# Feed-forward entry: the first two weight blocks interleaved by rows of tiles, squares summed in pairs before the matrix engine

## The chip, the cores and the metric

The kernel runs on one core of a Trainium2 chip, as one launch. The metric is the device time of that launch in microseconds. All times here are of this kernel on this kind of chip.

## The reference, cut to what matters

The program is a two-layer trunk with three sub-layers per layer: a feed-forward (F1), a token mixer, and a second feed-forward (F2). All three start with a norm of the residual stream and end with another. The change touches only how a feed-forward starts.

```
def rmsnorm(x, g):
    y = xf * lax.rsqrt(jnp.mean(xf * xf, axis=-1, keepdims=True) + RMS_EPS)
    return (y * g.astype(jnp.float32)).astype(x.dtype)
def swiglu(x, wg, wu, wd):
    return (jax.nn.silu(x @ wg) * (x @ wu)) @ wd
for l in range(DEPTH):                      # DEPTH = 2
    h = swiglu(rmsnorm(x, ffn1_pre_g[l]), ffn1_wg[l], ffn1_wu[l], ffn1_wd[l])
    x = x + 0.5 * rmsnorm(h, ffn1_post_g[l])
    m, new = token_mix(rmsnorm(x, mix_pre_g[l]), l, ...)
    x = x + rmsnorm(m, mix_post_g[l])
    h = swiglu(rmsnorm(x, ffn2_pre_g[l]), ffn2_wg[l], ffn2_wu[l], ffn2_wd[l])
    x = x + 0.5 * rmsnorm(h, ffn2_post_g[l])
```

The model width is 1024, the feed-forward width 2816, and there are T = 320 tokens (256 of a prompt, 64 of samples). Everything is float32.

## The kernel before, in words

**Layout.** The residual `x` lies in on-chip memory transposed: 8 tiles of 128 rows (channels) by 320 columns (tokens). A weight block is 128 x 2048 numbers, which is 8 tiles along the input channels (k = 0 to 7) times 256 output channels (two halves, c = 0 and 1). Blocks are streamed through two buffers `raw[0]` and `raw[1]` by the SP queue, each load waiting until the block before in the same buffer was used up (`lo_ready`).

**Split numbers.** A product of two float32 numbers is made of three products of a reduced format: high weights by high input, high weights by low input, low weights by high input. ScalarE (ACT) rounds a block to its high part `whi[s]` (`split_hi`, counted by `hi_ready`), VectorE (DVE) subtracts to get the low part `wlo[s]` (`split_lo`, counted by `lo_ready`). Likewise ACT writes `uh` (x times gain, rounded; `high_input`) and DVE writes `ul` (the rest; `low_input`). A feed-forward block is thus 16 tiles (c, k) by 3 = 48 matmuls of TensorE (PE) into the two PSUM banks `dps[:, 2s]` and `dps[:, 2s + 1]`.

**The norm is applied late.** The inputs `uh`, `ul` are not yet divided by the root of the mean square. ACT also writes the squares of x into `u` (`square`, two tiles at a time, counted by `sq_ready`). PE multiplies them by a matrix of ones into `mx[:, 3]` (`pre_sum`, line 659: two matmuls of ordinary float32 after each group of tiles, eight in all). The last one signals `sum_done`; ACT takes the root (`root`), DVE takes the reciprocal (`scale`, line 1480) and only then scales what came out of the first block (`times_scale`, line 1422).

**The entry of a feed-forward.** The inputs come in four groups j = 0 to 3 of two tiles, because DVE and ACT are still making them (`border` and `enter`: DVE scales and adds the sub-layer before to x, ACT rounds, DVE subtracts). PE works on block 0 in the order of the groups: for each j, wait for `u_ready`, 12 matmuls, then `pre_sum`. After all of block 0 it takes block 1, 48 matmuls, then a loop over the other upper blocks (2 to 21), then 12 lower ones. While PE is in block 1, the following chain runs for block 2, in this order on DVE: `scale`, `times_scale` of block 0's result, `split_lo` of block 2. PE may start block 2 when that last one is done. Four entries occur in the program: F1 and F2 of both layers. Between the last matmul of the sub-layer before and an entry, `keep_busy` issues 11 matmuls whose result is not used.

**Engines wait by semaphores alone**; every engine's order is the order of the code. POOL's queue waits for the `sum_done` of F1 to start loading small weights and the first halves of blocks for the mixer.

Of the kernel before, what the change touches and what calls it, by code (L numbers as in the profile page):

```python
# [27 lines left out]
ALU = mybir.AluOpType  # L28
# [3 lines left out]
P = 128  # L32
D = 1024
KD = D // P
# [4 lines left out]
T = TP + NB * TS  # L39
# [13 lines left out]
NFF = 2 * (B_A - B_F1)  # L53
# [93 lines left out]
def trunk(nc, xT, wstream, smallw, params, logits, consts, st_shift, st_rwkv, st_lru, st_conv, st_hgrn,  # L147
          yT, o_shift, o_rwkv, o_lru, o_conv, o_hgrn):
    ctx = ExitStack()
    with ctx:  # L150
# [212 lines left out]
        def wait_turn(eng, l, g):  # L363

            eng.wait_ge(S["turn_done"], l * NTURN + (g + 1))

        def landed(l, pair):

            return (l * NLOAD + pair - ((B_G0 - B_B) // 2 if 2 * pair >= B_G0 else 0)) * 16 + 16
# [170 lines left out]
        def _(pe):  # L540
# [7 lines left out]
            def pair_wait(l, qhalf, s):  # L548

                pe.wait_ge(pair_free[s], l * (NPAIR // 2) + qhalf + 1)  # L550
# [99 lines left out]
            def keep_busy(n):  # L650

                for _ in range(n):
                    pe.matmul(mx[:, 2, 0:2 * P], ident, cst[:, 0:2 * P], start=True, stop=True)

            def pre_sum(l, idx, j):

                pe.wait_ge(S["sq_ready"], l * 24 + (4 * idx + j + 1))
                for k in (2 * j, 2 * j + 1):
                    m = pe.matmul(mx[:, 3, 0:T], ones, u[:, k, :], start=k == 0, stop=k == KD - 1,  # L659
                                  skip_group_check=True)  # L660
                if j == 3:
                    m.then_inc(S["sum_done"], 1)

            def added_sum(l, idx):

                pe.wait_ge(S["sq_added"], l * 3 + (idx // 2 + 1))
                pe.matmul(mx[:, 3, 0:T], ones, sq[:, 0, :], start=True, stop=False, skip_group_check=True)

            def next_sum(l, idx):
# [18 lines left out]
            def split_tiles(s, kt, hi, lo_, half, first=True, last=True, k0=0, norm=None, ends=None):  # L688
# [6 lines left out]
                for c, k, j in order:  # L695
# [14 lines left out]
                    if norm and c == 1 and k == 2 * j + 1:  # L710
                        pre_sum(norm[0], 2 * norm[1], j)

            def ffn(l, b, q, f):
                def split_in(i, j):

                    pe.wait_ge(S["lo_ready"], l * NFF + i * 2 + (B_A * f + j + 3))

                for s in range(2):
                    split_in(0, s)
                    pair_wait(l, q // 2, s)  # L720
                    split_tiles(s, KD, uh[:, :, :], ul[:, :, :], s, norm=None if s else (l, 2 * f))
                with pe.Fori(1, KF // 2) as i:
                    for s in range(2):
                        split_in(i, s)
                        pair_wait(l, i + q // 2, s)
                        split_tiles(s, KD, uh[:, :, :], ul[:, :, :], s)
                for j in range(12):
                    half, part = j // 3, j % 3
                    pe.wait_ge(S["lo_ready"], l * NFF + (B_A * f + KF + j + 3))
                    if part == 0:  # L730
                        pair_wait(l, (q + KF + half) // 2, half % 2)

                    pe.wait_ge(S["h_ready"], l * 22 + (11 * f + 1 + (4, 8, 11)[part]))
                    split_tiles(j % 2, 8 if part < 2 else 6, hfh, hfl, half % 2, first=part == 0, last=part == 2,
                                k0=8 * part, ends=(l, 4 * f + 1) if j == 11 else None)
                post_sum(l, 4 * f + 1)
# [680 lines left out]
        def _(dve):  # L1417
            def tt(out, a, b, op):
                return nc.vector.tensor_tensor(out, a, b, op)  # L1419
# [84 lines left out]
            def add_squares(l, idx, j):  # L1504
# [6 lines left out]
                if j == 2:  # L1511
                    m.then_inc(S["sq_added"], 1)

            def border(l, idx, step, following):

                def scaled(j):

                    k = slice(2 * j, 2 * j + 2)
                    times_scale(ho[:, k, :], ho[:, k, :])
                    fence()  # L1520

                def renew(k):

                    return stt(x[:, k, :], ho[:, k, :], step, x[:, k, :], ALU.mult, ALU.add)

                scale(l, idx)
                for k in range(2):
                    mul(ho[:, k, :], ho[:, k, :], rs[:, :])
                    fence()
                    renew(k).then_inc(S["x_new" if k else "x_first"], 1)  # L1530
                for j in range(4):
                    if j == 0 and following:
                        low_input(*following, j, lambda: scaled(1))
                    else:
                        if j < 3:
                            scaled(j + 1)
                        if following:
                            low_input(*following, j)
                    if j < 3:
                        renew(slice(2 * j + 2, 2 * j + 4)).then_inc(S["x_new"], 1)  # L1540

            def split_lo(l, f, i, j, s):

                dve.wait_ge(S["hi_ready"], l * NFF + i * 2 + (B_A * f + j + 1))
                tt(wlo[s][:, :], raw[s][:, :], whi[s][:, :].bitcast(F32), ALU.subtract).then_inc(S["lo_ready"], 1)
# [426 lines left out]
            for l in range(L):  # L1972
                nc.vector.tensor_copy(prm[:, :], tile_at(prm_all, l)).then_inc(S["prm_ready"], 1)
                if l == 0:
                    for j in range(4):
                        low_input(0, 0, "ffn1_pre_g", j)
                    split_lo(0, 0, 0, 0, 0)
                ffn(l, B_F1, 0)
                if l == 0:
                    dve.wait_ge(S["const_loaded"], 16)  # L1980
# [215 lines left out]
```

## Time and profile before

| what | us |
|---|---|
| median of 3 runs | 2083.63 |
| lowest and highest of them | 2079.86, 2084.89 |
| the profiled execution, its time | 2080.08 |
| the profiled execution, its span | 2078.3 |
| TensorE busy in it | 2037.3 (98%) |
| VectorE busy in it | 1379.3 (66%) |
| ScalarE busy in it | 797.3 (38%) |

The span is from the first to the last instruction of the profiled execution; 1.8 us of its time lie around it. In rows of the profile a matmul is shown with its full duration, but the next one starts before it ends; the useful number is the distance from start to start.

### The profile page before, as it was taken

To read this page: it belongs to the slowest core of one execution; us is meant where nothing else is said; L and a number is where in the kernel's file an instruction comes from. 1 tells how busy PE (TensorE), PEld (TensorE's weight loads), DVE (VectorE), ACT (ScalarE), POOL (GpSimd) and SP (SyncE) were. 2 spreads that over 40 slices of the span, in tenths; PEclk is the share of its full clock that TensorE was granted. 3 is DMA by queue.
4 is the path that set the end of the run, shared out by engine and by line. 5 is a ranking of instruction groups with operands and counts; after the bars stand their busy time and mean duration, and the time that the engine had idled before them with its cause. 6 is when DMAs were issued, how large, how long until landed. Compare 5 with 4: busy or idle time off the path is not lost.

```text
span 2078.3 us, 31983 instructions
## 1 busy us (share of the span) xinstructions
PE 2037.3 (98%) x12928; PEld 1868.1 (90%) x12928; DVE 1379.3 (66%) x2053; ACT 797.3 (38%) x940; POOL 86.1 (4%) x164
## 2 busy tenths in 40 slices
PE   7999999999999999999999999999999999999998
PEld 6999989888877798999999998989887778989998
DVE  5776487877667676555377755877874676766544
ACT  4444463333243244233354444623323323443332
POOL 1111000000000000000011100000000000000000
PEclk9999999999999999999999999999999999999999
DMA  6887423333332342444458864323333333434442
GB/s 239 304 308 266 172 107 108 113 113 112 125 122 104 123 174 102 143 160 151 167 193 309 297 241 160 129 88 113 113 113 132 107 122 143 142 115 148 161 146 102
DMA packets 60826, 326.66 MB, mean 157 GB/s; under 512 B 7249, under 2 KB 7441, under 8 KB 34481
## 3 DMA queue, kind: packets, MB, share of 16 engines
q1 hardware_dynamic: 43200, 262.92, 35.9%
q0 software_dynamic: 17520, 62.27, 8.2%
q8 instruction: 75, 1.23, 0.2%
q14 instruction: 31, 0.25, 0.0%
HBM read 290.81 MB, written 34.36 MB: 156 GB/s over the span
## 4 chain that ended last, share of the span: by engine, by line
PE 92%; DVE 4%; DVEq 1%; ACT 1%; DMA 1%; issue 1%; SPq 0%
PE dps L703 44%; PE dps L607 11%; PE dps L557 10%; PE dps L642 6%; PE mx L803 2%; PE mx L817 2%; PE mx L813 2%; PE mx L917 2%; PE mx L659 1%; PE dps L630 1%; DMA raw<-in_wstream 1%; DVE ho L1422 1%; PE mx L933 1%; PE mx L760 1%; PE mx L970 1%; PE mx L947 1%
## 5 line engine op out<-in xcount | busy, mean ns | idle before, releaser
L1047 ACT ACTIVATE whi<-raw 128x2048 fp32r<-128x2048 f32 (+1 forms) x144 | 269.1, 1869 | 486.2 <-PE dps L703 465.0
L1419 DVE TENSOR_TENSOR wlo<-raw,whi 128x2048 fp32r<-128x2048 f32 x136 | 311.7, 2292 | 210.2 <-ACT whi L1047 205.2
L703 PE MATMUL dps<-uh,whi 128*128 128x320 f32 x1408 | 430.3, 306 | 19.6 <-DVE wlo L1419 15.0
L703 PE MATMUL dps<-uh,wlo 128*128 128x320 f32 x1408 | 434.3, 308 | 0.0
L703 PE MATMUL dps<-ul,whi 128*128 128x320 f32 x1408 | 432.9, 307 | 0.0
L703 PEld LDWEIGHTS dps<-uh,whi 128*128 128x128 f32 x1408 | 264.8, 188 | 25.1 <-issue 18.4
L703 PEld LDWEIGHTS dps<-uh,wlo 128*128 128x128 f32 x1408 | 264.8, 188 | 0.0
L703 PEld LDWEIGHTS dps<-ul,whi 128*128 128x128 f32 x1408 | 264.0, 187 | 0.6
L607 PE MATMUL dps<-u,raw 128*128 128x320 f32 x768 | 234.5, 442 | 0.0
L703 PE MATMUL dps<-hfh,whi 128*128 128x320 f32 x704 | 220.4, 313 | 0.0
L703 PE MATMUL dps<-hfh,wlo 128*128 128x320 f32 x704 | 217.6, 309 | 0.0
L703 PE MATMUL dps<-hfl,whi 128*128 128x320 f32 x704 | 216.7, 308 | 0.0
L642 PE MATMUL dps<-nh,parts 128*128 128x320 f32 x704 | 211.0, 342 | 0.0
L607 PEld LDWEIGHTS dps<-u,raw 128*128 128x128 f32 x768 | 137.9, 191 | 50.6 <-issue 5.3
L703 PEld LDWEIGHTS dps<-hfl,whi 128*128 128x128 f32 x704 | 133.2, 189 | 0.6
L703 PEld LDWEIGHTS dps<-hfh,whi 128*128 128x128 f32 x704 | 132.3, 188 | 0.6
L703 PEld LDWEIGHTS dps<-hfh,wlo 128*128 128x128 f32 x704 | 132.0, 187 | 0.0
L642 PEld LDWEIGHTS dps<-nh,parts 128*128 128x128 f32 x704 | 126.8, 189 | 4.1 <-issue 2.9
L1047 ACT ACTIVATE tmp<-mx 128x640 f32<-128x640 f32 (+2 forms) x80 | 47.4, 592 | 194.8 <-PE mx L803 127.7
L1422 DVE TENSOR_TENSOR ov<-dps,ov 128x640 f32<-128x640 f32 x52 | 42.8, 823 | 71.9 <-PE dps L703 65.9
L1047 ACT ACT_TABLE_LOAD x64 | 82.1, 1283 | 2.1 <-PEq L2177 0.7
L1422 DVE TENSOR_TENSOR ov<-dps,rs 128x640 f32<-128x640 f32 x56 | 46.2, 824 | 54.3 <-PE dps L703 45.3
(321 smaller groups left out, 3493.3 us busy)
## 6 DMA issues: line engine op xcount, KB each, us to landing
raw<-in_wstream SPq DMA_DIRECT2D x198, 1024.0 KB, 4.8
u<-in_wstream POOLq DMA_DIRECT2D x44, 512.0 KB, 7.1
split_store<-wha POOLq DMA_DIRECT2D x44, 512.0 KB, 7.6
raw<-in_wstream SPq DMA_DIRECT2D x44, 512.0 KB, 4.1
parts<-split_store SPq DMA_DIRECT2D x44, 512.0 KB, 5.0
hs<-in_st_hgrn POOLq DMA_DIRECT2D x8, 512.0 KB, 5.6
out_o_hgrn<-hs POOLq DMA_DIRECT2D x8, 512.0 KB, 2.9
out_yT<-x SPq DMA_DIRECT2D x2, 1280.0 KB, 4.5
```

The costliest lines, as they stand in the source:

```text
L557: m = pe.matmul(out, w[:, k, n0:n0 + P], v[:, k, :], start=first and i == 0, stop=last and i == 2, skip_group_check=True)
L607: m = pe.matmul(dps[:, 2 * s + c, 0:T], w[:, k, c * P:(c + 1) * P], u[:, k, :], start=k == 0, stop=k == KD - 1, skip_group_check=True)
L630: m = pe.matmul(dps[:, 2 * (b % 2) + c, 0:T], w[:, k, c * P:(c + 1) * P], u[:, k, :], start=k == 0, stop=k == KD - 1, skip_group_check=True)
L642: m = pe.matmul(dps[:, 2 * (b % 2) + c, 0:T], w[:, k % 4, c * P:(c + 1) * P], v, start=k == 0 and t == 0, stop=k == KD - 1 and t == 2, ski ...
L703: m = pe.matmul(dps[:, 2 * half + c, 0:T], w[:, k, c * P:(c + 1) * P], v[:, k0 + k, :], start=first and k == 0 and i == 0, stop=last and k ...
L803: m = pe.matmul(mx01[:, c * P:(c + 1) * P], ao[li % 2][:, c, :], tinv[:, c, :], start=True, stop=True)
L813: m = pe.matmul(mx23[:, c * P:(c + 1) * P], tinvt[:, c, :], zs[:, c, :], start=True, stop=True)
L817: m = pe.matmul(product_at(li, c), zs[:, c, :], tinvt[:, c, :], start=True, stop=True)
L917: m = pe.matmul(mx[0:b - a, (li + 1) % 2, a:b], kss[li % 2][:, a:b], qps[li % 2][:, a:b], start=True, stop=True)
L1047: return nc.scalar.activation(out, in_, f, **kw)
L1419: return nc.vector.tensor_tensor(out, a, b, op)
L1422: return nc.vector.tensor_tensor(out, a, b, ALU.mult)
```

## The change

Block 0 and block 1 are worked on together at the entry of every feed-forward, by the new function `entry`. After group j of block 0 (12 matmuls), PE does the same group of block 1 with the high weights only (8 matmuls: 4 tiles by `uh` and `ul`). The low weights of block 1 (16 matmuls) come after all of that. The sums of squares are no longer made from eight tiles: DVE first adds two tiles of `u` to one (`add_pair`, signalled by `sq_added`), and PE multiplies only the four results by ones (`pair_sum`), one after group 1 of block 0, one after group 2, two after group 3. Numbers counted by `sq_added` elsewhere are shifted to fit.

```
--- before.py
+++ after.py
@@ -363,6 +363,14 @@
         def wait_turn(eng, l, g):
 
             eng.wait_ge(S["turn_done"], l * NTURN + (g + 1))
+
+        def pair_added(l, idx, j):
+
+            return l * 11 + ((0, 6)[idx // 4] + j + 1)
+
+        def post_added(l, idx):
+
+            return l * 11 + {1: 5, 3: 6, 5: 11}[idx]
 
         def landed(l, pair):
 
@@ -652,6 +660,13 @@
                 for _ in range(n):
                     pe.matmul(mx[:, 2, 0:2 * P], ident, cst[:, 0:2 * P], start=True, stop=True)
 
+            def pair_sum(l, idx, j):
+
+                pe.wait_ge(S["sq_added"], pair_added(l, idx, j))
+                m = pe.matmul(mx[:, 3, 0:T], ones, u[:, 2 * j, :], start=j == 0, stop=j == 3, skip_group_check=True)
+                if j == 3:
+                    m.then_inc(S["sum_done"], 1)
+
             def pre_sum(l, idx, j):
 
                 pe.wait_ge(S["sq_ready"], l * 24 + (4 * idx + j + 1))
@@ -663,7 +678,7 @@
 
             def added_sum(l, idx):
 
-                pe.wait_ge(S["sq_added"], l * 3 + (idx // 2 + 1))
+                pe.wait_ge(S["sq_added"], post_added(l, idx))
                 pe.matmul(mx[:, 3, 0:T], ones, sq[:, 0, :], start=True, stop=False, skip_group_check=True)
 
             def next_sum(l, idx):
@@ -710,15 +725,48 @@
                     if norm and c == 1 and k == 2 * j + 1:
                         pre_sum(norm[0], 2 * norm[1], j)
 
+            def entry(l, q, f):
+
+                tiles = [[v[s][:, :].rearrange("p (k n) -> p k n", k=KD) for v in (whi, wlo)] for s in range(2)]
+
+                def part(s, c, k, w, v, first, last):
+
+                    return pe.matmul(dps[:, 2 * s + c, 0:T], tiles[s][w][:, k, c * P:(c + 1) * P], v[:, k, :],
+                                     start=first, stop=last, skip_group_check=True)
+
+                pe.wait_ge(S["lo_ready"], l * NFF + (B_A * f + 3))
+                pair_wait(l, q // 2, 0)
+                for j in range(4):
+                    ks = (2 * j, 2 * j + 1)
+                    for c, k in [(c, k) for k in ks for c in range(2)] if j == 0 else [(c, k) for c in range(2) for k in ks]:
+                        if c == 0 and (k == 2 * j or k == 1):
+                            u_wait(l, 2 * f, k)
+                        part(0, c, k, 0, uh, k == 0, False)
+                        part(0, c, k, 0, ul, False, False)
+                        m = part(0, c, k, 1, uh, False, k == KD - 1)
+                    if j == 3:
+                        m.then_inc(S["block_done"], 1)
+                    if j == 0:
+                        pe.wait_ge(S["hi_ready"], l * NFF + (B_A * f + 2))
+                        pair_wait(l, q // 2, 1)
+                    for i in (() if j == 0 else (j - 1,) if j < 3 else (2, 3)):
+                        pair_sum(l, 4 * f, i)
+                    for c in range(2):
+                        for k in ks:
+                            part(1, c, k, 0, uh, k == 0, False)
+                            part(1, c, k, 0, ul, False, False)
+                pe.wait_ge(S["lo_ready"], l * NFF + (B_A * f + 4))
+                for c in range(2):
+                    for k in range(KD):
+                        m = part(1, c, k, 1, uh, False, k == KD - 1)
+                m.then_inc(S["block_done"], 1)
+
             def ffn(l, b, q, f):
                 def split_in(i, j):
 
                     pe.wait_ge(S["lo_ready"], l * NFF + i * 2 + (B_A * f + j + 3))
 
-                for s in range(2):
-                    split_in(0, s)
-                    pair_wait(l, q // 2, s)
-                    split_tiles(s, KD, uh[:, :, :], ul[:, :, :], s, norm=None if s else (l, 2 * f))
+                entry(l, q, f)
                 with pe.Fori(1, KF // 2) as i:
                     for s in range(2):
                         split_in(i, s)
@@ -1511,6 +1559,11 @@
                 if j == 2:
                     m.then_inc(S["sq_added"], 1)
 
+            def add_pair(l, n, j):
+
+                dve.wait_ge(S["sq_ready"], l * 24 + (8 * n + j + 1))
+                tt(u[:, 2 * j, :], u[:, 2 * j, :], u[:, 2 * j + 1, :], ALU.add).then_inc(S["sq_added"], 1)
+
             def border(l, idx, step, following):
 
                 def scaled(j):
@@ -1538,6 +1591,10 @@
                             low_input(*following, j)
                     if j < 3:
                         renew(slice(2 * j + 2, 2 * j + 4)).then_inc(S["x_new"], 1)
+                    if following and following[1] != 1 and j:
+                        add_pair(*following[:2], j - 1)
+                if following and following[1] != 1:
+                    add_pair(*following[:2], 3)
 
             def split_lo(l, f, i, j, s):
 
@@ -1975,6 +2032,8 @@
                     for j in range(4):
                         low_input(0, 0, "ffn1_pre_g", j)
                     split_lo(0, 0, 0, 0, 0)
+                    for j in range(4):
+                        add_pair(0, 0, j)
                 ffn(l, B_F1, 0)
                 if l == 0:
                     dve.wait_ge(S["const_loaded"], 16)
```

The rows below are the program's instruction order on one engine. A name as `dps<-uh,whi` is the tile written and the tiles read, `mx<-u,cst` is a sum of squares by ones. First PE, at the end of block 0 of a feed-forward's entry before the change:

```order
L703 MATMUL dps<-uh,wlo 128x320
L659 MATMUL mx<-u,cst 128x320 [waits sq_ready]
L659 MATMUL mx<-u,cst 128x320
L703 MATMUL dps<-uh,whi 128x320 [waits pair_free1,lo_ready]
L703 MATMUL dps<-ul,whi 128x320
```

The last two rows begin block 1, whose 48 matmuls all stand behind the last sum. PE at the same place in the change, from the end of group 3 of block 0 to the start of block 2:

```order
L734 MATMUL dps<-uh,wlo 128x320
L666 MATMUL mx<-u,cst 128x320 [waits sq_added] x2
L734 MATMUL dps<-uh,whi 128x320
L734 MATMUL dps<-ul,whi 128x320
L734 MATMUL dps<-uh,whi 128x320
L734 MATMUL dps<-ul,whi 128x320
L734 MATMUL dps<-uh,whi 128x320
L734 MATMUL dps<-ul,whi 128x320
L734 MATMUL dps<-uh,whi 128x320
L734 MATMUL dps<-ul,whi 128x320
L734 MATMUL dps<-uh,wlo 128x320 [waits lo_ready]
L734 MATMUL dps<-uh,wlo 128x320 x15
```

Behind the last sum there now stand 8 matmuls with high weights and 16 with low ones, and then block 2; the other 24 of block 1 have moved ahead of it. The new wait in the entry is at the first group of block 1, which needs its high weights. PE in the change, from the end of group 0 of block 0:

```order
L734 MATMUL dps<-uh,wlo 128x320
L734 MATMUL dps<-uh,whi 128x320 [waits pair_free1,hi_ready]
L734 MATMUL dps<-ul,whi 128x320
L734 MATMUL dps<-uh,whi 128x320
L734 MATMUL dps<-ul,whi 128x320
L734 MATMUL dps<-uh,whi 128x320
L734 MATMUL dps<-ul,whi 128x320
L734 MATMUL dps<-uh,whi 128x320
L734 MATMUL dps<-ul,whi 128x320
L734 MATMUL dps<-uh,whi 128x320 [waits u_ready]
```

Where two sums stood between the groups, eight matmuls of block 1 stand now. On DVE at the program's start, the rows before the change:

```order
L1419 TENSOR_TENSOR wlo<-raw,whi 128x2048 [waits hi_ready] x2
L1480 RECIPROCAL rs<-rt 128x320 [waits rt_ready]
L1422 TENSOR_TENSOR ov<-dps,rs 128x640 [waits block_done]
L1419 TENSOR_TENSOR wlo<-raw,whi 128x2048 [waits hi_ready]
L1422 TENSOR_TENSOR ov<-dps,ov 128x640 [waits block_done,silu_ready]
```

and in the change:

```order
L1467 TENSOR_TENSOR wlo<-raw,whi 128x2048 [waits hi_ready]
L1467 TENSOR_TENSOR u<-u 128x320 [waits sq_ready] x4
L1467 TENSOR_TENSOR wlo<-raw,whi 128x2048 [waits hi_ready]
L1528 RECIPROCAL rs<-rt 128x320 [waits rt_ready]
L1470 TENSOR_TENSOR ov<-dps,rs 128x640 [waits block_done]
L1467 TENSOR_TENSOR wlo<-raw,whi 128x2048 [waits hi_ready]
```

The four additions stand between the low weights of block 0 and those of block 1; the reciprocal, the scaling and the low weights of block 2 keep their order. At the other three entries two of the four additions stand between the steps that make the inputs, and two right ahead of the low weights of block 1.

## Rows read from the trace of the kernel before

**Rows 1.** The page: busy time by engine, and the chain that ended last.

```profile
PE 2037.3 (98%) x12928; PEld 1868.1 (90%) x12928; DVE 1379.3 (66%) x2053; ACT 797.3 (38%) x940; POOL 86.1 (4%) x164
...
PE 92%; DVE 4%; DVEq 1%; ACT 1%; DMA 1%; issue 1%; SPq 0%
```

**Rows 2.** Waits of PE: in total us, times, longest.

```profile
PE dps L703 <- DVE wlo L1419: 15.0, 1, 15.0
PE dps L703 <- DVE ul L1425: 4.6, 9, 0.8
```

**Rows 3.** Timeline of PE, third entry (F1, layer 2): start, us, instruction.

```profile
1046.82 1.24 PE L659 MATMUL mx<-u,cst 128*128 128x320 f32 x4
1048.67 0.41 PE L703 MATMUL dps<-uh,whi 128*128 128x320 f32 x1 [0.61 <-DVE ul L1425]
1048.92 0.31 PE L703 MATMUL dps<-ul,whi 128*128 128x320 f32 x1
...
1056.19 1.24 PE L659 MATMUL mx<-u,cst 128*128 128x320 f32 x4
1057.41 0.31 PE L703 MATMUL dps<-ul,whi 128*128 128x320 f32 x1
...
1064.21 0.30 PE L703 MATMUL dps<-uh,whi 128*128 128x320 f32 x1
```

**Rows 4.** Timelines of ACT and DVE around the same entry.

```profile
1053.13 0.72 ACT L1047 ACTIVATE u<-x 128x640 f32<-128x640 f32 x1
1057.47 0.53 ACT L1047 ACTIVATE rt<-mx,epst 128x320 f32<-128x320 f32 x1 [3.61 <-PE mx L659]
...
1041.90 0.49 DVE L1422 TENSOR_TENSOR ho<-ho,rs 128x320 f32<-128x320 f32 x1
...
1047.60 1.01 DVE L1425 SCALAR_TENSOR_TENSOR ul<-x,prm_all,uh 128x320 fp32r<-128x320 f32 x2 [0.34 <-ACT uh L1047]
...
1050.43 1.01 DVE L1425 SCALAR_TENSOR_TENSOR ul<-x,prm_all,uh 128x320 fp32r<-128x320 f32 x2 [0.35 <-ACT uh L1047]
...
1054.33 2.28 DVE L1419 TENSOR_TENSOR wlo<-raw,whi 128x2048 fp32r<-128x2048 f32 x1
1058.03 2.15 DVE L1480 RECIPROCAL rs<-rt 128x320 f32<-128x320 f32 x1 [1.42 <-ACT rt L1047]
1060.25 0.82 DVE L1422 TENSOR_TENSOR ov<-dps,rs 128x640 f32<-128x640 f32 x1
1060.99 2.28 DVE L1419 TENSOR_TENSOR wlo<-raw,whi 128x2048 fp32r<-128x2048 f32 x1
```

**Rows 5.** Timelines of PE, ACT and DVE at the first entry (program start).

```profile
27.97 0.55 PE L703 MATMUL dps<-uh,whi 128*128 128x320 f32 x1
28.36 0.31 PE L703 MATMUL dps<-ul,whi 128*128 128x320 f32 x1
...
30.37 1.90 ACT L1047 ACTIVATE whi<-raw 128x2048 fp32r<-128x2048 f32 x1
...
32.30 2.29 DVE L1419 TENSOR_TENSOR wlo<-raw,whi 128x2048 fp32r<-128x2048 f32 x1 [0.27 <-ACT whi L1047]
```

**Rows 6.** Third entry, later: ACT and DVE for blocks 4 and 5.

```profile
1072.61 1.92 ACT L1047 ACTIVATE whi<-raw 128x2048 fp32r<-128x2048 f32 x1 [6.23 <-DMA raw<-in_wstream]
...
1074.56 2.29 DVE L1419 TENSOR_TENSOR wlo<-raw,whi 128x2048 fp32r<-128x2048 f32 x1 [2.40 <-ACT whi L1047]
...
1082.53 2.29 DVE L1419 TENSOR_TENSOR wlo<-raw,whi 128x2048 fp32r<-128x2048 f32 x1
```

**Rows 7.** Windows in the mixer: PE, PEld, DVE, ACT, POOL, granted clock, DMA, GB/s.

```profile
708.50:711.90 3.40, 3.40 (x23) 2.46 (x21) 1.22 (x1) 0.00 (x0) 1.03 (x2) 1.00 0.46 193
711.95:715.36 3.41, 3.41 (x10) 2.48 (x10) 0.00 (x0) 2.05 (x3) 0.00 (x0) 0.50 0.44 173
```

**Rows 8.** Timeline of PE from 711.6 us on.

```profile
711.62 1.14 PE L947 MATMUL mx<-tmp,hs 128*128 128x8 f32 x6
712.60 3.22 PE L607 MATMUL dps<-u,raw 128*128 128x320 f32 x6
```

## The prediction

> **What bounds the kernel now.** I read the page first: TensorE is busy 98% of the span and is 92% of the chain that ended last [rows 1]. Then the waits of PE: apart from 15.0 us before its first matmul, the largest group is 4.6 us in nine waits for `ul`, the low inputs that VectorE makes at the entries [rows 2]; no wait for low weights occurs behind the first one. So PE bounds nearly everything, and an edit is worth what it takes from PE's own stream or from a wait there, unless it makes a new wait. Then I read the timeline of PE at the third entry, which the second and fourth repeat to 0.1 us with other offsets. The reader is to see in it three things. The four passes of a pair of sums take the place from 1056.19 to 1057.41 - 0.145 = 1057.27, so 1.08 us, or 0.54 us for one sum [rows 3]. Matmuls of split numbers follow each other in (1064.21 - 1057.41) / 47 = 0.145 us [rows 3], so a block of 48 is 6.95 us. And after group 0 PE stands until 1048.67, because the low inputs of group 1 come then; the stream goes on as if it had begun at 1048.92 - 0.145 = 1048.78 [rows 3]: a restart costs 0.17 us from what released it, low inputs that end at 1047.60 + 1.01 = 1048.61 [rows 4].
>
> The last view is the chain that runs beside block 1. The last sum ends at 1057.27; root at 1057.47, reciprocal at 1058.03, scaling at 1060.25, low weights of block 2 from 1060.99 to 1063.27 [rows 4]. That is 6.01 us from sum to weights. PE has 6.95 us of block 1 to do meanwhile and begins block 2 at 1064.21, so this chain has a slack of only 0.9 us. At the first entry it is longer: the last sum ends at 28.36 - 0.145 = 28.21, ACT loads a table first and has the high weights of block 2 at 32.27, the low ones end at 34.59 [rows 5], which is 6.38 us; the slack is 0.6.
>
> **The change part by part.** *The sums.* Four of eight go: 4 x 0.54 = 2.15 us less of PE per entry, 8.6 us for four.
>
> *Filling the wait after group 0.* Two sums (1.08 us) are replaced by 8 matmuls (1.16), so PE comes free at 1047.98 and still waits to 1048.78. That hides 0.1 us of the stall and no more, since the waited-for tiles do not come earlier.
>
> *The additions on VectorE.* No row shows this very operation. The nearest is a product of 128x320 at 0.49 us [rows 4]. Below, nothing, where VectorE waits anyway; above, four times 0.49 = 2.0 us per entry if all lay on the path. I take 0.1 us of effect on the inputs: the first addition stands between the renewal of x and the next scaling, and pushes the inputs of group 2, ready at 1051.4 now [rows 4], to 1051.6. PE comes to group 2 at 1052.2 in the new order (below), so this is covered by 0.6 us. The other three move the low weights of block 1 from 1054.33 to about 1055.3, done at 1057.6 [rows 4]; PE wants them only at 1059.6. The last squares are there at 1053.85 [rows 4], so the last addition is done by 1055.3 and its sum, at 1057.4, does not wait either. Without these covers an addition would cost its 0.49. The new wait for high weights of block 1 costs nothing: in ACT's code order they stand ahead of the inputs (`split_hi` before `enter`).
>
> *PE in the new order, third entry.* From 1048.78: group 1 of block 0 (12 x 0.145 = 1.74) to 1050.52, a sum to 1051.06, 8 of block 1 (1.16) to 1052.22; group 2 to 1053.96, sum to 1054.50, 8 to 1055.66; group 3 to 1057.40, two sums to 1058.48. Here is the step on which all rests: the last sum now ends 1.2 us later than before (1057.27), since 24 matmuls (3.48 us) of block 1 have moved ahead of it and only 2.15 us of sums and 0.1 of stall went. Behind it stand 8 + 16 = 24 matmuls, to 1061.96. That would be the gain, 2.25 us.
>
> *The chain.* It still needs 6.01 us from the last sum, now with 3.48 us of PE's work beside it and not 6.95. The low weights of block 2 are ready at 1058.48 + 6.01 = 1064.49, and with the restart of 0.17 block 2 begins at 1064.66, where it began at 1064.21. So PE stalls 2.7 us, the 2.25 are all given back, and 0.45 us more. At the first entry the last sum moves by 3.48 - 2.15 = 1.33 to 29.55, weights at 35.93, block 2 at 36.10 where it was 28.21 + 6.95 = 35.17: 0.93 us more, with a stall of 3.1. Sum over four entries: 0.93 + 3 x 0.45 = 2.3 us slower.
>
> *What is late next.* At the third entry the load of block 4 is issued behind the low weights of block 2, and ACT waits for it until 1072.61; from there VectorE has no slack, so that the low weights of block 5 end at 1084.82 [rows 6], 0.24 before PE's block 5 (1064.21 + 3 x 6.95 = 1085.06). If the load moves with its issue by 1.2 us, block 5 starts at 1086.02 + 0.17 and not at 1085.06 + 0.45: 0.7 us more. Bounds are nothing (if the load's lateness belongs to this execution) and 0.7; I take 0.7. Behind that VectorE follows PE. The queue of POOL, which waits for the same sum in F1, starts 1.2 to 1.3 us later; what it loads is for the mixer, and the waits of PE name none of it. Sum: 3.0 us.
>
> *The clock.* The trace before has no stall of PE as long as 2.7 us once it runs, so what one does to the granted clock is not seen. It has one fall: in 711.95 to 715.36 the granted clock is 0.50, which is 1.2 GHz and not 2.4, and in the stretch ahead, at 1.00, PE ended with a series of matmuls of 8 columns [rows 7, 8]. In the low stretch six float32 matmuls take 3.22 us [rows 8], some 0.53 each, where they take 0.27 at full clock [rows 3]: PE does half of its work, and 3.41 us at half cost 1.7. PE was never idle there, it only had little to stream; a stall of 2.7 us has nothing to stream. Bounds per stall: nothing, and 1.7 us; for four stalls nothing to 6.8. Since a mere thinning of the stream was enough once, I take it that the clock falls after about two of the four stalls, one of them partly under the stall itself: 2.5 us.
>
> The Trainium skill speaks to this (TensorE: Matmul & The Clock Gate, "HAM oscillation — how this bites in real kernels"): it names a length of idle gap below which the clock is not expected to fall, and the stalls worked out here are shorter. By that rule the sum would be 3.0 us; by the row of the fall it is 5.5. No row here shows a gap of this length, but the fall in the rows came with no gap at all, which speaks against taking the rule as sufficient.
>
> Together: 3.0 + 2.5 = 5.5 us slower than the profiled execution's 2080.08. That execution is near the lowest of three whose mean is (2079.86 + 2083.63 + 2084.89) / 3 = 2082.8; they differ by 5 us among themselves. I put the difference on that mean: 2088.3 us. What a measurement of this kernel can tell from no change is about 0.3%, which is 6.2 us; the forecast is within it.
>
> **The rivals.** *The clock holds.* Only the stalls and the late load count: +2.3 to 3.0, 2085.8 us. For it: no gap of this length in the trace shows a fall. Against: the one fall had less reason.
>
> *The clock falls after every stall, or more waits follow.* 3.0 + 6.8 = 9.8, 2092.6 us. For it: all four stalls are alike. Against: one fall is all that the rows show, and a fall that begins inside a stall is partly hidden by it.
>
> *Faster.* The chain behind the last sum does not hold block 2, and the 2.25 us per entry stay: 9 us, 2073.8. This is so if the chain takes less than 3.48 us; it begins to pay from 1064.21 - 0.17 - 1058.48 = 5.56 us. It has 6.01, made of instructions that the change leaves alone (0.53, 2.15, 0.82, 2.28 and what lies between), so it would need the last sum to end 0.45 us earlier than I work out.
>
> *The change does little.* If PE stalled for the additions, the sum would be later still; if the extra work of VectorE pushed the inputs, each of three groups would cost up to 0.5. Both add to the slower side and are held by the upper bound.
>
> **How the numbers follow.** Forecast (stalls, clock falls after one to three) 0.44, from 3.0 + 1.7 to 3.0 + 5.1, so 2087.5 to 2091. Clock holds 0.30. Falls after all, or further waits, 0.19. Faster 0.07, spread between -9 us and a gain too small to tell. The range leaves out most of the last two: from 2082, the clock-holding case less the unevenness of the runs, to 2094. Within 0.3%: the clock-holding case (0.29), two thirds of the forecast (0.28) and part of the faster one (0.02), 0.59. Slower by more: the other third of the forecast (0.16), all falls or further waits (0.19) and 0.01 of the clock-holding case, 0.36. Faster by more: 0.05.
>
> **What the profile after would show.** The rows of sums by ones at the entries halve: four entries with 8 passes and not 16. The waits of PE should name the low weights of blocks after the first, three times 2.5 to 2.7 us and once about 3.0, each right behind 16 matmuls of `uh,wlo`. The root of the third entry should begin 1.2 us later against the entry's start, and the additions in VectorE's timeline should be about 0.45 us each. If block 2 begins at once behind those 16 matmuls, the step of the chain is wrong. If the stalls are there and the granted clock of the stretches behind them is 1.00, the term of 2.5 us is wrong and 2085.8 is the better number. If the inputs of groups 2 and 3 are waited for, I have mis-sized the additions.

## The result and the profile after

| | before | after |
|---|---|---|
| median, us | 2082.44 (11 runs) | 2088.01 (11 runs) |
| lowest and highest, us | 2079.86, 2084.89 | 2087.29, 2091.64 |
| profiled execution: time, span, us | 2080.08, 2078.3 | 2087.66, 2085.9 |

The ratio is 1.0029, with a 95% interval of 1.0021 to 1.0038. The change makes the kernel slower, by 5.6 us after the medians and by 6.0 us after the ratio (4.4 to 7.9). The interval leaves out a ratio of 1, so the direction is sure, though the size is about what was named as hard to tell.

The waits of PE in the changed kernel (in total us, times, longest) have one group that the kernel before does not have [rows 2]:

```profile
PE dps L734 <- DVE wlo L1467: 14.8, 1, 14.8
PE dps L718 <- DVE wlo L1467: 10.2, 4, 2.8
PE dps L734 <- DVE ul L1473: 4.4, 9, 0.8
```

Line 718 is the loop over the later blocks. Four times, once per entry, PE stands and waits for the low weights of block 2: 2.84 us at the first entry and 2.46 to 2.47 us at the others. The waits for inputs fell from 4.6 to 4.4 us only. The timeline of PE at the third entry, against [rows 3]:

```profile
1047.89 0.39 PE L734 MATMUL dps<-uh,whi 128*128 128x320 f32 x1 [0.73 <-DVE ul L1473]
...
1052.00 0.41 PE L734 MATMUL dps<-uh,whi 128*128 128x320 f32 x1 [0.51 <-DVE ul L1473]
...
1060.77 1.24 PE L666 MATMUL mx<-u,cst 128*128 128x320 f32 x4
1061.60 0.55 PE L734 MATMUL dps<-uh,whi 128*128 128x320 f32 x1
1061.99 0.31 PE L734 MATMUL dps<-ul,whi 128*128 128x320 f32 x1
...
1063.02 2.51 PE L734 MATMUL dps<-uh,wlo 128*128 128x320 f32 x16
1067.99 0.41 PE L718 MATMUL dps<-uh,whi 128*128 128x320 f32 x1 [2.47 <-DVE wlo L1467]
```

The entry's first matmul is the first row, at 1047.89; before the change it was at 1044.56, so 3.33 us are to be taken off to compare. The last sum then ends at 1061.99 - 0.145 - 3.33 = 1058.51 (1057.27 before, 1058.48 predicted), the sixteen low matmuls are done 3.5 us later, and block 2 begins at 1064.66, where the forecast put it; before it began at 1064.21. That it fits to the hundredth is luck: the weights end 0.04 us later than forecast, and the first matmul starts 0.13 us behind them, where 0.17 was taken for the restart. The chain on ACT and DVE, against [rows 4]:

```profile
1062.05 0.53 ACT L1095 ACTIVATE rt<-mx,epst 128x320 f32<-128x320 f32 x1 [4.72 <-PE mx L666]
...
1057.66 0.89 DVE L1467 TENSOR_TENSOR u<-u 128x320 f32<-128x320 f32 x2
...
1058.60 2.28 DVE L1467 TENSOR_TENSOR wlo<-raw,whi 128x2048 fp32r<-128x2048 f32 x1
1062.61 2.15 DVE L1528 RECIPROCAL rs<-rt 128x320 f32<-128x320 f32 x1 [1.73 <-ACT rt L1095]
1064.83 0.82 DVE L1470 TENSOR_TENSOR ov<-dps,rs 128x640 f32<-128x640 f32 x1
1065.58 2.28 DVE L1467 TENSOR_TENSOR wlo<-raw,whi 128x2048 fp32r<-128x2048 f32 x1
```

From the last sum (1061.85) to the end of the low weights (1067.86) it is 6.01 us, as before. DVE itself idles 1.73 us for the root, so it is not the additions that hold it: they and the low weights of block 1 are done at 1060.88.

Windows of the changed kernel (PE, PEld, DVE, ACT, POOL, granted clock, DMA, GB/s): at the third entry the stretch ahead of block 2, the one behind it, and the next; then the stretches behind block 2's start at the second and the fourth entry:

```profile
1065.50:1068.40 2.90, 0.43 (x4) 0.41 (x4) 2.90 (x3) 2.72 (x3) 0.00 (x0) 1.00 0.87 331
1068.47:1071.88 3.41, 3.41 (x15) 3.41 (x14) 3.05 (x5) 0.00 (x0) 0.00 (x0) 0.50 1.01 382
1071.90:1075.30 3.40, 3.40 (x26) 3.40 (x24) 1.49 (x1) 0.00 (x0) 0.00 (x0) 1.00 0.85 287
...
822.71:826.13 3.42, 3.42 (x15) 3.42 (x14) 3.10 (x4) 0.00 (x0) 0.00 (x0) 0.50 0.85 292
1853.54:1856.95 3.41, 3.41 (x15) 3.41 (x14) 3.05 (x5) 0.00 (x0) 0.00 (x0) 0.50 0.74 257
```

Behind every stall the clock is granted at half, 1.2 GHz, for 3.4 us: 15 matmuls lie in that stretch where 26 lie in the one after it. The first entry has one such stretch too (37.65 to 41.06). All four begin 0.4 to 1.0 us after PE has taken up work again (1068.47 against 1067.99 at the third), so none of the slow time is hidden under the stall. Such a stretch is called a fall below.

The same reading at all entries shows what each costs. From the entry's first matmul, block 2 begins after 20.11, 20.10 and 20.10 us at the second to fourth entry (19.65 before, so 0.45 more each), and block 3 after 28.72, 28.71 and 28.72 (26.58, 26.59, 26.58 before). The fall thus costs 2.14 - 0.45 = 1.7 us each. At the first entry it is 21.87 against 20.18, and block 3 30.49 against 27.12. All four: 3.37 + 3 x 2.14 = 9.8 us.

### The profile page after: what moved, and what is told of

Its sections match the earlier page's. It is cut to its first block, busy times and chain, and to the rows that moved or that the text cites. A ratio compares the mean times of both kernels' runs of the same rounds, so it can differ in the third digit from the quotient of the medians.

```text
span 2085.9 us, 31935 instructions
## 1 busy us (share of the span) xinstructions
PE 2035.2 (98%) x12896; PEld 1869.5 (90%) x12896; DVE 1385.5 (66%) x2069; ACT 797.1 (38%) x940; POOL 86.1 (4%) x164
## 4 chain that ended last, share of the span: by engine, by line
PE 91%; DVE 5%; ACT 1%; DVEq 1%; DMA 1%; issue 1%; SPq 0%
PE dps L718 42%; PE dps L615 10%; PE dps L565 10%; PE dps L650 6%; PE mx L851 2%; PE mx L865 2%; PE dps L734 2%; PE mx L861 2%; PE mx L965 1%; DVE rs L1528 1%; PE dps L638 1%; DMA raw<-in_wstream 1%; DVE ho L1470 1%; PE mx L981 1%; PE mx L808 1%; PE mx L1018 1%
## 5 line engine op out<-in xcount | busy, mean ns | idle before, releaser
L718 PE MATMUL dps<-uh,whi 128*128 128x320 f32 x1280 | 390.6, 305 | 10.2 <-DVE wlo L1467 10.2
L718 PE MATMUL dps<-uh,wlo 128*128 128x320 f32 x1280 | 397.0, 310 | 0.0
L718 PE MATMUL dps<-ul,whi 128*128 128x320 f32 x1280 | 395.7, 309 | 0.0
L718 PEld LDWEIGHTS dps<-uh,whi 128*128 128x128 f32 x1280 | 242.7, 190 | 11.3 <-issue 11.3
L718 PEld LDWEIGHTS dps<-uh,wlo 128*128 128x128 f32 x1280 | 242.7, 190 | 0.0
L718 PEld LDWEIGHTS dps<-ul,whi 128*128 128x128 f32 x1280 | 241.9, 189 | 0.0
```

The source lines that it names most:

```text
L718: m = pe.matmul(dps[:, 2 * half + c, 0:T], w[:, k, c * P:(c + 1) * P], v[:, k0 + k, :], start=first and k == 0 and i == 0, stop=last and k ...
```

## The experiments

Each kernel was timed beside the kernel before on the same chip, or run once. The last two columns give the start of block 2 and of block 3, in us after the first matmul of the third entry; each number is the distance between two rows of a timeline. The second and fourth entry agree with the third to 0.03 us, except where the text says otherwise. The edits below are shortened: a comment stands for what is left out.

| kernel | median, us | kernel before there | ratio, 95% interval | block 2 of entry 3 after | block 3 after |
|---|---|---|---|---|---|
| before | | | | 19.65 | 26.59 |
| changed | 2088.01 | 2082.44 | 1.0029 (1.0021 to 1.0038) | 20.10 | 28.71 |
| stall filled | 2083.3 | 2081.14 | 1.0008 (0.9999 to 1.0017) | 20.12 | 27.17 |
| pairs only | 2078.34 | 2081.14 | 0.9988 (0.9979 to 0.9997) | 20.10 | 27.03 |
| rows only | 2094.86 | 2081.14 | 1.0063 (1.0048 to 1.0079) | 21.46 | 28.51 |
| early sum | 2075.39 | 2081.14 | 0.9973 (0.9963 to 0.9984) | 18.71 | 25.65 |
| high first | 2075.66 | 2082.63 | 0.9968 (0.9955 to 0.9980) | 17.91 | 25.03 |
| both | 2071.64 | 2082.63 | 0.9946 (0.9932 to 0.9959) | 17.58 | 24.61 |
| both, eight sums | 2080.63 | 2081.94 | 0.9990 (0.9981 to 0.9999) | 18.83 | 25.86 |
| before, high first | 2081.56 | 2081.94 | 1.0002 (0.9993 to 1.0012) | 19.65 | 26.68 |
| one filler | 2089.05 (one run) | 2082.63 | | 20.10 | 28.73 |
| changed, once more | 2088.56 (one run) | 2082.63 | | 20.12 | 28.74 |

**The stall filled.**

```
                         m = part(1, c, k, 1, uh, False, k == KD - 1)
                 m.then_inc(S["block_done"], 1)
+                keep_busy(5)
```

> The changed kernel with five more of the unused matmuls (128x256, float32) right behind the low weights of block 1 at each entry, where PE would stall for the low weights of block 2. Each takes 0.45 us where eleven of them fill the time ahead of an entry, so 2.2 us of the 2.5 us stall are filled, and nothing else moves. Theory one (the chain behind the last sum sets when block 2 starts, and the idle time lets the granted clock fall behind it): block 2 still starts 0.45 us later than before at the second to fourth entry, no stretch of 0.50 stands behind an entry, and the time is 2.3 to 3.1 us above the kernel before and 5 to 7 us below the changed one. Theory two (the falls come from the order or the reuse of weights, not from idling): the four stretches at 0.50 stay and the time is that of the changed kernel. Theory three (block 2 is held by something that the matmuls add to): later than the changed kernel by up to 9 us.

Timeline of PE, third entry (its first matmul is at 1046.46), and the window behind block 2's start:

```profile
1063.95 2.32 PE L661 MATMUL mx<-cst 128*128 128x256 f32 x10
1066.58 0.42 PE L718 MATMUL dps<-uh,whi 128*128 128x320 f32 x1 [0.31 <-DVE wlo L1468]
```

```profile
1067.00:1070.40 3.40, 3.40 (x25) 3.40 (x25) 3.05 (x5) 0.00 (x0) 0.00 (x0) 1.00 1.00 328
```

Block 2 begins at the same place and the clock holds behind all four entries, so theories two and three fall. The idling, not the order of the matmuls, brings the clock down. Theory one has the places right and its sizes only roughly: the kernel is 2.2 us slower than before by the medians and 1.7 by the ratio, whose interval takes in no difference, where 2.3 to 3.1 were expected; the excess of the changed kernel shrank by 3.4 us by the medians and 4.4 by the ratios, where 5 to 7 were expected. At the entries the whole 6.2 us are there (block 3 begins 1.60 us earlier than in the changed kernel at the first, 1.54 to 1.56 at the others). What takes part of them back lies in the mixer: this kernel's profile has two falls there, the changed kernel's none.

**The sums of pairs alone, and the order alone.** The first puts block 1 whole behind block 0 again, behind a wait for its low weights; the second takes the additions out:

```
-                    for c in range(2):                       # in the loop over the groups
-                        for k in ks:
-                            part(1, c, k, 0, uh, k == 0, False)
-                            part(1, c, k, 0, ul, False, False)
+                for c in range(2):                           # behind it
+                    for k in range(KD):
+                        part(1, c, k, 0, uh, k == 0, False)
+                        part(1, c, k, 0, ul, False, False)
+                        m = part(1, c, k, 1, uh, False, k == KD - 1)
```

> The change with the sums of pairs alone: VectorE's additions and four sums, but block 1 whole behind block 0 as before. My theory: at the second to fourth entry the inputs set the pace, so the last sum ends at the same time as before (within 0.2 us), and block 1 then waits for its low weights, which the additions push by 0.9 us: block 2 about 0.5 us later per entry; at the first entry, where the inputs are there, 2.15 us are gained. In all -1 to 0 us against before, with no stretch at 0.50 behind an entry. Rival (four sums less are four sums gained): 8.6 us faster than before.

```
-                    for i in (() if j == 0 else (j - 1,) if j < 3 else (2, 3)):
-                        pair_sum(l, 4 * f, i)
+                    pre_sum(l, 4 * f, j)
-                        add_pair(*following[:2], j - 1)      # and the other calls of add_pair
```

> The change with the order alone: block 1 interleaved with high weights first, but eight sums made from the squares and no addition. My theory: the last sum ends 2.6 us later than before (8 matmuls more in each of three groups, less the 0.9 us stall that they fill), block 2 starts about 1.8 us later at entries two to four and 3.1 us later at the first, with a stall of about 2.6 us at each and a stretch of 3.4 us at 0.50 behind each: 8.5 + 6.8 = 15 us slower than before. Rival (it is the additions that make the chain late): about as fast as before, with no stall ahead of block 2.

Pairs alone gain a little, 2.5 us by the ratio (0.6 to 4.4): more than my -1 to 0 but far from 8.6. At the entries the gain is only 0.25 us in all (block 3 begins 1.34 us earlier at the first and 0.32, 0.45 and 0.32 later at the others), as expected, and the profiled execution is 1.0 us faster than that of the kernel before; the rest of the ratio comes from outside the entries. At the third entry three waits for inputs have taken the place of the sums (block 2 begins 0.45 us later than before). The last sum ends only 0.14 us later than before, and block 1 then starts at 1056.09, 0.06 us behind the end of its low weights and 0.3 us later than behind the sum alone; about 0.5 had been expected for this wait. The three waits for inputs:

```profile
1047.16 0.41 PE L734 MATMUL dps<-uh,whi 128*128 128x320 f32 x1 [1.69 <-DVE ul L1469]
1050.11 0.41 PE L734 MATMUL dps<-uh,whi 128*128 128x320 f32 x1 [0.41 <-DVE ul L1469]
1052.95 0.42 PE L734 MATMUL dps<-uh,whi 128*128 128x320 f32 x1 [0.29 <-DVE ul L1469]
```

The order alone costs 13 us by the ratio: block 2 begins 1.8 us later, as worked out, with a stall of 2.46 us, so the lateness is the order's and not the additions'. Against the expectation, the clock fell behind two of the four stalls only, those of the first and the fourth entry (block 3 of the fourth begins 30.04 us after its first matmul, and not 28.51). The windows behind the stalls of the second and the fourth entry:

```profile
829.30:832.70 3.40, 3.40 (x23) 3.40 (x24) 3.05 (x5) 0.21 (x1) 0.00 (x0) 1.00 0.65 210
...
1862.00:1865.30 3.30, 3.29 (x12) 3.30 (x13) 2.95 (x5) 0.25 (x1) 0.00 (x0) 0.50 0.57 199
```

Its profiled execution has besides a stall of 2.79 us in the mixer, where ACT waited 6.67 us for a load, with one more fall behind it; it is part of its high span of 2094.7 us. No other profile here has a wait above 0.4 us at that line. Whether the order brings it about is not shown.

**How long a stall, and the changed kernel once more.** The first has one filler for five; the second has no edit.

```
-                keep_busy(5)
+                keep_busy(1)
```

> The changed kernel with one unused matmul (128x256, float32) behind the low weights of block 1 at each entry: 0.45 us of the stall filled, so that PE idles some 2.0 us there and not 2.5. Block 2 starts where it did. It asks how long a stall has to be: if a stall of 2.0 us is still followed by a lower clock, some of the four entries show a stretch at 0.50 behind them; if the clock holds as it did behind the waits of 1.7 us of the kernel with pairs alone, none do and the time is near 2083.

> The changed kernel once more, for a second look: the four stalls of 2.5 and 2.8 us are there again to 0.05 us. If a stall of 2.5 us is always followed by a lower clock there are four stretches at 0.50 behind entries; if it is only often so, as the kernel with rows alone shows with two of four, there are one to three, and the time between 2084 and 2088 goes with their number, 1.7 us each.

With one filler PE idles 2.03 to 2.04 us at entries two to four (2.41 at the first), and the clock still falls behind each, so the case in which it holds is out:

```profile
824.94:828.34 3.40, 3.40 (x15) 3.40 (x14) 3.16 (x3) 0.00 (x0) 0.00 (x0) 0.50 0.74 294
1855.76:1859.16 3.40, 3.40 (x15) 3.40 (x14) 3.14 (x4) 0.00 (x0) 0.00 (x0) 0.50 0.73 289
```

The changed kernel run once more shows four falls at the entries too, so for this kernel the first of the two cases holds. Falls were seen behind 14 of 16 stalls of 2.0 to 2.8 us at entries (four each in the two profiles of the changed kernel and in that of the one-filler kernel, two of four with rows alone), and behind none of the three waits of 1.7 us of the kernel with pairs alone.

**An early sum.** Only group 0 of block 1 goes ahead, and the last two sums move into group 3:

```
+                        if j == 3 and n == 2:                # behind 9 of the 12 matmuls of group 3
+                            pair_sum(l, 4 * f, 2)
+                            pair_sum(l, 4 * f, 3)
-                        for k in ks:
+                    for k in ks if j == 0 else range(2, KD) if j == 3 else ():
```

> Same work as the changed kernel, another order: only group 0 of block 1 goes ahead; the last two sums stand inside group 3 of block 0; the other high weights of block 1 follow behind them, low weights last. My theory: the last sum ends near 1056.8 on the scale of the trace before (1057.3 there), the low weights of block 2 end near 1062.9, and PE comes to block 2 at about 1063.1, so 1.0 us earlier than before per entry and 1.8 us at the first: 4 to 5 us faster than before, about 10 us faster than the changed kernel, with no stretch at 0.50 behind an entry. Rival (the gain of the sums was never there, or the additions eat it): within 1 us of the kernel before.

**High weights first in blocks 2 and 3.** On the changed kernel; the loop begins one turn later:

```
+                for s in range(2):
+                    high_first(l, q, f, s)    # wait hi_ready and pair_free, 32 matmuls with whi,
+                                              # wait lo_ready, 16 with wlo, block_done
-                with pe.Fori(1, KF // 2) as i:
+                with pe.Fori(2, KF // 2) as i:
```

> The changed kernel, and blocks 2 and 3 too begin with their high weights, low ones last, so that block 2 no longer stands behind the 2.28 us of its low weights but only behind the scaling. If the chain from the last sum to the low weights of block 2 is what takes the gain back, block 2 can start 3.8 us (root to scaling) and 0.17 behind the last sum, so 1.7 to 1.8 us earlier than in the kernel before at each entry, with a stall of 0.5 us where the changed kernel has 2.5 and no stretch at 0.50 behind it: 7 us faster than before, 12 us faster than the changed kernel. Rival (something else holds block 2, such as the banks of PSUM or the high weights): no better than the filled kernel, 2083.

**Both.** The early sum and high weights first, and four matmuls of block 1 behind each of the sums of groups 1 and 2. Against the early sum, beside `high_first`:

```
-                    for k in ks if j == 0 else range(2, KD) if j == 3 else ():
+                    for k in ks if j == 0 else (j + 1,) if j < 3 else range(4, KD):
```

> The order with the early sum (sums inside group 3), the two short waits for the inputs of groups 2 and 3 each filled by four matmuls of block 1, and blocks 2 and 3 with high weights first. PE should have no wait but those for the inputs: block 2 starts 2.15 to 2.2 us earlier than before at each entry, 8.7 us in all, near 2072.5. Rival (VectorE becomes the bound and a wait comes back at block 3 or 4): like the early-sum kernel, 2075 to 2076.

All three are faster than before, by 5.6, 6.7 and 11.2 us after their ratios, where 4 to 5, 7 and 8.7 were expected. At the third entry block 2 begins 0.94, 1.74 and 2.07 us earlier (1.0, 1.7 to 1.8, 2.15 to 2.2 expected), so the mechanism is confirmed there. At the first it begins 2.28, 1.13 and 1.52 us earlier; how long the slow clock of the program's start lasts has a part in these three (see below). Up to the start of block 5 the four entries gain 5.0, 4.3 and 6.6 us in all; what the ratios of the last two show beyond lies outside the entries. The timeline of the high-first kernel at block 2 of the third entry (line 772; the entry's first matmul at 1042.63) shows what releases it now:

```profile
1057.76 2.51 PE L734 MATMUL dps<-uh,wlo 128*128 128x320 f32 x16
1060.54 0.39 PE L772 MATMUL dps<-uh,whi 128*128 128x320 f32 x1 [0.28 <-DVE ov L1489]
```

It is the scaling, as meant. At the first entry it is the high weights of block 2, which come later than the scaling there (its first matmul is at 14.76):

```profile
33.81 0.41 PE L772 MATMUL dps<-uh,whi 128*128 128x320 f32 x1 [0.43 <-ACT whi L1114]
```

The kernel with both (first matmul at 1039.61), where nothing is waited for right ahead of block 2:

```profile
1054.84 2.50 PE L734 MATMUL dps<-uh,wlo 128*128 128x320 f32 x16
...
1057.18 0.31 PE L776 MATMUL dps<-uh,whi 128*128 128x320 f32 x1
```

It is the fastest version here, 0.54% (0.41 to 0.68%) under the kernel before.

**The eight sums in that order, and a control.** The one is the version with both with `pre_sum` and without `add_pair`, the other the kernel before with `high_first` for blocks 2 and 3 (the edit of the high-first kernel on another base).

```
-                            pair_sum(l, 4 * f, 2)
-                            pair_sum(l, 4 * f, 3)
-                    elif j < 3:
-                        pair_sum(l, 4 * f, j - 1)
+                    pre_sum(l, 4 * f, j)                     # behind each group
```

> The fastest order so far (early groups of block 1 interleaved, blocks 2 and 3 with high weights first) with the eight sums of the kernel before and no additions on VectorE. It prices the sums where nothing behind them takes the gain back. By my working the eight sums fill 0.8 us that otherwise is waiting for inputs, so they cost 1.2 us per entry at the second to fourth and 2.15 us at the first: 5.7 us slower than the version with four sums, near 2077.5. Rival (four sums less are 2.15 us at every entry): 8.6 us slower, 2080. Rival (the additions on VectorE cost as much as they save): no difference, 2072.

> A control: the kernel before, with blocks 2 and 3 beginning with their high weights and nothing else changed. There the low weights of block 2 are ready 0.9 us before PE comes to them, so the chain is not on the path and freeing it should be worth nothing: within 0.5 us of the kernel before, block 2 of the second to fourth entry 19.65 us after the entry's first matmul as before. Rival (high weights first is a gain in itself): 2 to 7 us faster.

At the entries the eight sums cost 18.83 - 17.58 = 1.25 us and 20.84 - 18.66 = 2.2 us at the first, so 5.9 us, and the spans of the two profiled executions differ by 2079.0 - 2073.3 = 5.7. The ratios differ by more (0.44%, 9 us), which is near the rival's 8.6; but the rival has 2.15 us at every entry, and that is seen at the first only. The rest lies outside the entries. The control has the ratio 1.0002 (0.9993 to 1.0012), and block 2 begins where it did: freeing the chain is worth nothing where it has slack.

## Why the prediction was right

The mechanism was right, and so was the total; that the total is so near is luck. The term for the clock was 4.3 us too low, the first entry 0.8 too low and the late load 0.7 too high, and something outside the entries made up for the 4 us. In turn:

*Sums, fill, additions, chain.* All were right, and the start of block 2 at entries two to four too (+0.45 predicted, +0.45 and +0.46 measured). The additions took 0.48 us each, the low weights of block 1 were done before PE wanted them. That the order and not the additions makes the sum late is shown by the rows-only kernel; that the chain behind the sum takes the gain back is shown by the high-first kernel, which leaves the chain as it is and lets block 2 begin ahead of its last link: there, at entries two to four, it begins 1.7 us earlier than before.

*The first entry* was mis-sized: +0.93 predicted, +1.69 measured. Its last sum came 2.1 us later and not 1.3, because the matmuls at the start kept their slow distance of 0.27 us until about 20.6, where before it ended at about 19.0: 1.6 us more at half speed are the 0.8 us that the forecast lacks. When the changed kernel ran once more the slow distance ended by 18.6 and the start of block 2 was +0.73. So when this slow beginning ends varies between executions of one kernel, and the change is not needed to explain it.

*What is late next* (0.7 us for the load of block 4) did not come: the load landed 6.7 us behind its issue in the changed kernel's profile, not 9.1 as in the profile before, and block 5 of the third entry begins as far behind block 3 as at the others. The lower of its two bounds was right. Where blocks come faster the late load returns: in the version with both, block 5 of the third entry begins 0.3 us later than that of the second.

*The clock* was mis-sized the other way, and this is the largest error: two falls of four, one of them partly under its stall, with 2.5 us in all were taken, and the clock fell behind all four, with nothing hidden, for 4 x 1.7 = 6.8 us. The rival "after every stall" was right about the entries. The mechanism is shown by the filled kernel: same start of block 2, no fall, and block 3 begins 1.54 us earlier than in the changed kernel at the third entry. By the medians the excess over the kernel before goes from 5.6 to 2.2 us.

*So the total fits better than its terms.* The terms at the entries add up to 9.8 us where 5.5 was forecast and 5.6 is the difference of the medians. Between the profiled executions it is 7.6: from block 21 of the first entry to the second entry the changed kernel's took 2.0 us less, since it has no fall in the mixer, where the one of before has that of [rows 7]; the changed kernel run once more has one at 714.78 and is 0.9 us longer. The kernel before had a lucky execution in its profile, 2080.08 against a median of 2082.44, while the changed kernel's 2087.66 is near its median; so 7.6 - 2.4 + 0.4 = 5.6. The control, which has the entries of the kernel before to 0.2 us each, shows two falls in the mixer twice as long:

```profile
711.46:718.28 6.82, 6.82 (x18) 4.86 (x18) 0.45 (x1) 3.06 (x5) 0.26 (x1) 0.50 0.22 87
1742.29:1749.11 6.82, 6.82 (x17) 4.71 (x17) 0.74 (x1) 3.35 (x5) 0.10 (x1) 0.50 0.22 87
```

Over the twelve profiles the falls in the mixers add up to between 0 (the changed kernel) and 13.6 us (the control), which is worth 0 to 6.8 us. With half their length and the shift at the entries up to block 5 the difference of each profiled span from that of the kernel before comes out to 0.8 us, but for the kernel with rows alone, whose stall in the mixer is the other 2.5. The timed executions bear this out: of the 55 of the kernel before that ran beside the experiments, the 31 with a mean granted clock of 0.998 took 2080.3 to 2082.7 us and the 11 with 0.996 took 2083.3 to 2085.8. All eleven of the changed kernel have 0.994 to 0.996, four falls at the entries included. So falls in the mixer can be the 4 us between the entries' 9.8 and the medians' 5.6. Whether the changed kernel has them less often than the kernel before, and why, stays open: one or two profiles per kernel and a clock to the thousandth, which is 2 us, do not count them.

## What to carry to other kernels

Before work is pulled forward to fill a wait, ask what it is pulled ahead of: here it was a sum that starts a chain on two other engines, and to have that early was worth more than to fill the wait of 0.9 us behind group 0. The slack of the chain (here 0.9 us) is the budget of such a move; once it is used up, work taken from the tail, where it covered the chain, is paid back one for one. Then either start the chain earlier or let the work behind it begin with what does not need its last link; at the second to fourth entry both were worth what the rows said, to 0.1 us. And where one execution differs from the next by falls of the clock elsewhere, compare distances inside the changed stretch, and not totals alone.

## What the runs showed of the hardware that was not expected

At the entries a stall of TensorE of 2.0 to 2.8 us was followed by a stretch of 3.4 us at a granted clock of 0.50, which is 1.2 GHz, in 14 of 16 cases, where PE had been busy until the stall; the Trainium skill (TensorE: Matmul & The Clock Gate, "HAM oscillation — how this bites in real kernels") puts the idle gap that does this higher, and here the measurement decides. Two stalls of 2.46 us in one execution (rows alone, second and third entry) had no fall behind them, so that length alone does not settle it. Five unused matmuls of 2.3 us in all in such a stall bought back 1.54 to 1.60 us per entry. In the mixer falls came without a stall of this length too ([rows 7]), and their total varies from 0 to 13.6 us between the profiles.
